# One selection over seven score tiles in place of two interleaved groups, in the odd layer of a hybrid decoder

## The chip, the cores and the metric

The kernel runs on one core of one Trainium2 chip. The metric is the device time of one execution in microseconds; the median of the runs shown is compared. The whole program is one launch.

## The reference, cut to what matters

One inference step of a two-layer trunk: 1024 prompt tokens and 32 sample tokens (8 requests of 4) go through the same weights. The odd layer has an indexer-sparse attention. Each query scores all keys with a small indexer, keeps the 256 best of them (129 of the 516 of a sample query), and attends to these alone:

```python
def _dsa_select(iq, iw, ik, qpos, kpos, ksel):
    r = jax.nn.relu(jnp.einsum('bthd,bsd->bhts', iq, ik))
    score = jnp.einsum('bhts,bth->bts', r, iw)
    score = jnp.where(kpos[None, :] <= qpos[:, None], score, NEG)
    val, idx = lax.top_k(score, ksel)
    return idx, val > 0.5 * NEG
...
        idx, valid = _dsa_select(iqb, iwb, ik, qpos, kpos, ksel)
        g = kv[bidx, idx]
        s = jnp.einsum('bthgd,btshd->bhgts', qb, g[:, :, :, 0]) * SCALE
        p = _masked_softmax(s, valid[:, None, None])
        return jnp.einsum('bhgts,btshd->bthgd', p, g[:, :, :, 1])
```

## The kernel before, in words

`trunk` runs the even layer, then the odd one: `dense` (input projection), `dsa`, `dense` (output projection "oo"), norms and feed-forward. The change lies in `dsa` (L1929), the helper `index_scores` (L2027) and the class `Selection` (L2130).

**The tiles.** The prompt has NT = 8 tiles j of 128 queries; a query of tile j sees (j+1)*128 keys. Tiles 0 and 1 see at most 256 keys and need no selection, so `first` = 2. Tiles 2 to 7 have score tiles of 384, 512, 640, 768, 896 and 1024 columns in `best`; the sample queries have one of 32 rows by 544 columns, `best_s`. These are the seven score tiles.

**The selection.** `Selection` finds each row's threshold by a bitwise search of 31 rounds. `start` counts the scores at or above zero, works out signs and ranks in small operations, and writes sign-flipped copies (`flip`). Each round (`step`) sets one bit of the candidate `cand` (L2202), counts for each tile the copies under it (L2210, a compare with an accumulated sum, on DVE), compares the counts with the limits (`keep`, L2215) and takes over the bit (L2216). `link` makes DVE wait for its own last instruction. For tiles marked `on_act` the count is made on ACT instead (`signs`, L2226, a Sign with accumulator): ACT waits for the candidate (`tried`), DVE's `keep` waits for ACT (`signed`). The last round counts all tiles on DVE. `finish` (L2233 to L2247) breaks ties with a running sum and turns the scores in `best` into a mask of 0 and NEG.

**The order.** `index_scores` goes through units (j, head): PE multiplies into one of two PSUM buffers, ACT takes the relu (L2103), DVE adds the weighted heads (L2120, L2122) and the causal mask (L2127). Every engine does its instructions in program order. The seven tiles are in two groups: group 0 is tiles 2 to 5 (2 and 3 counted on ACT), group 1 is tiles 6, 7 and the sample (7 on ACT); `half` = 6. In `index_scores`, from tile 6 on, DVE does group 0's `start` and one round ahead of each of the 12 units. The rest goes into `attend_prompt` (L778), the attention over all tiles. It goes through units u: tile 0 is one unit, tile 1 two, tiles 2 to 7 four each, 27 in all. PE makes the scores of unit u (L846), then turns (L863) and multiplies with the values (L878) the probabilities of unit u-2, in chunks of two key blocks; DVE adds the mask and takes the maximum (L920), `shift` (L928) releases ACT's exponentials (L999), DVE takes the reciprocal (L937), POOL scales (L978), ACT copies the turned chunks (L989), and DVE copies each tile's result out (L954). Scores of unit u wait for the mask step of two blocks before (two PSUM banks). `beside`, called ahead of `mask(u)` on DVE, and `beside_act` on ACT put the rounds in: beside tiles 0 and 1 the other 19 rounds of group 0 and its `finish`; beside tiles 2 to 5 group 1's `start`, 31 rounds and `finish`. Then SP, which waits for `chosen_sem`, fetches 32 pages of the key/value cache (L670) into the room that the selections used; `attend_samples` (from L1061) reads them behind `attend_prompt`.

Of the kernel before, what the change touches and what calls it, by code (L numbers as in the profile page):

```python
# [20 lines left out]
P = 128  # L21
# [1907 lines left out]
def dsa(nc, k, idx_rows):  # L1929


    with Stage(nc, "dsa") as st:
# [43 lines left out]
        index_scores(nc, k, idx_rows, index, iw, causal, best, best_s, first, at, half, selections[0])  # L1976
        pages = gather.rows
        bits = [chosen.bit for chosen in selections]
        chosen_sem = st.sem("chosen")

        def beside(dve, link, j, n, of):

            if j >= half:
                return
            m, lo, hi = (0, 0, first) if j < first else (1, first, half)
            chosen = selections[m]
            work = lambda x: (x * (x + 1) - lo * (lo + 1)) / (hi * (hi + 1) - lo * (lo + 1))
            before = lambda v: round(bits[m] * (work(j) + (work(j + 1) - work(j)) * v / of))
            if j == lo and n == 0 and m == 1:
                chosen.start(dve, link)  # L1990
            for _ in range(before(n), before(n + 1)):
                chosen.step(dve, link)
            if j == hi - 1 and n == of - 1:
                chosen.finish(dve, link)
                dve.sem_inc(chosen_sem, 1)

        def beside_act(act, j, n, of):

            if j >= half:
                return  # L2000
            m, lo, hi = (0, 0, first) if j < first else (1, first, half)
            chosen = selections[m]
            work = lambda x: (x * (x + 1) - lo * (lo + 1)) / (hi * (hi + 1) - lo * (lo + 1))
            before = lambda v: round(bits[m] * (work(j) + (work(j + 1) - work(j)) * v / of))
            for _ in range(before(n), before(n + 1)):
# [21 lines left out]
def index_scores(nc, k, gather, index, iw, causal, best, best_s, first, at, half, chosen):  # L2027


    with Stage(nc, "idx") as st:  # L2030
# [23 lines left out]
        with nc.Block() as block:  # L2054
# [36 lines left out]
            def _(act):  # L2091
# [7 lines left out]
                for n, (j, hh) in enumerate(units):  # L2099
# [4 lines left out]
                    if j >= half:  # L2104
                        chosen.signs(act)

            @block.vector
            def _(dve):
                link = Chain(dve, chain_sem)
                dve.wait_ge(loaded, 16)  # L2110
                for n, (j, hh) in enumerate(units):
                    r = rows(j)
                    if j == half and hh == 0:
                        chosen.start(dve, link)
                    if j >= half:
                        chosen.step(dve, link)
# [13 lines left out]
class Selection:  # L2130
# [10 lines left out]
    @staticmethod  # L2141
# [5 lines left out]
    def __init__(self, st, name, tiles, want, width, room):  # L2147

        flip, hits, self.cum, self.one = room
        self.lo, n = tiles[0][2], len(tiles)  # L2150
        self.want, self.width = want[:, self.lo:self.lo + n], width[:, self.lo:self.lo + n]
        self.tiles, at = [], 0
# [308 lines left out]
```

## Time and profile before

| | us |
|---|---|
| median of 3 runs (lowest, highest) | 3558.7 (3558.47, 3560.22) |
| profiled execution | 3561.3 |
| its span | 3559.7 |
| index scores and 12 rounds, 2162 to 2242 | 80 |
| attention beside the selections, 2242.5 to 2475 | 232 |
| attention of tiles 6 and 7 alone, 2475 to 2539 | 64 |

Over the span PE is busy 88%, DVE 46%, ACT 22%, POOL 7%; the mean granted clock is 0.908. PEclk is the granted TensorE clock as a share of full speed: 1.00 is 2.4 GHz and 0.50 is 1.2 GHz. The stages around the change are read stage by stage, since the mean shares hide that the engines change places. In a timeline row stand the start, the duration, the engine, the line, the operation and its operands, and in brackets the idle time ahead of it and what ended that. Starts are counted from the start of the span.

### The profile page before, as it was taken

The page shows a single profiled execution, that of the slowest core. Times are in us where ns is not written, and L with a number is a line of the kernel's source. Part 1 is how long each engine was busy: PE and PEld are TensorE (multiplying, and loading weights), DVE is VectorE, ACT ScalarE, POOL GpSimd, SP SyncE. Part 2 cuts the span into 40 slices and gives each one's busy share as a digit, 9 for nine tenths or more (in the row PEclk, how much of TensorE's full clock was granted, in tenths as well). Part 3 has the DMA queues.
Part 4 walks back from the last instruction along what each step waited for, and adds up shares of the span by engine and source line. Part 5 has one row for each costly group of instructions (what it writes and reads, how often), then busy time and mean ns, then how long its engine had stood idle before and what let it go on. Part 6 is the DMA issues. An engine that isn't in the chain of part 4 may idle for free. (4 is left out here: it accounts for less than half of the span.)

```text
span 3559.7 us, 49762 instructions
## 1 busy us (share of the span) xinstructions
PE 3117.9 (88%) x19939; PEld 2790.9 (78%) x19939; DVE 1626.1 (46%) x3131; ACT 797.7 (22%) x1551; POOL 248.1 (7%) x279
## 2 busy tenths in 40 slices
PE   8997799969879999999997968155897999999997
PEld 8997566548859999999986955033495999999995
DVE  2112287656444443344344245988335343344335
ACT  2110276523131000000003113454404000000002
POOL 2001000023000000000002720011100000000000
PEclk9999899977889999999998985567898999999998
DMA  6222310131202011111102330000111111001101
GB/s 232 99 86 102 110 38 1 42 123 31 68 12 83 36 49 36 60 36 36 48 1 75 118 105 0 0 1 15 45 36 36 60 48 60 36 36 48 59 13 49
DMA packets 63277, 193.46 MB, mean 54 GB/s; under 512 B 7812, under 2 KB 32292, under 8 KB 53792
## 3 DMA queue, kind: packets, MB, share of 16 engines
q1 hardware_dynamic: 58176, 172.86, 13.8%
q0 software_dynamic: 3904, 12.46, 1.1%
q10 hardware_dynamic: 1008, 5.41, 0.4%
q8 instruction: 145, 2.38, 0.3%
q14 instruction: 44, 0.36, 0.0%
HBM read 159.68 MB, written 35.36 MB: 55 GB/s over the span
## 5 line engine op out<-in xcount | busy, mean ns | idle before, releaser
L163 PE MATMUL f_up<-f_x_high,f_w_high 128*128 128x352 f32 x2112 | 686.3, 325 | 62.6 <-DVE f_x_low L638 48.5
L165 PE MATMUL f_up<-f_x_high,f_w_low 128*128 128x352 f32 x2112 | 681.5, 323 | 0.0
L164 PE MATMUL f_up<-f_x_low,f_w_high 128*128 128x352 f32 x2112 | 681.4, 323 | 0.0
L163 PEld LDWEIGHTS f_up<-f_x_high,f_w_high 128*128 128x128 f32 x2112 | 399.8, 189 | 65.5 <-issue 65.5
L164 PEld LDWEIGHTS f_up<-f_x_low,f_w_high 128*128 128x128 f32 x2112 | 400.4, 190 | 0.0
L165 PEld LDWEIGHTS f_up<-f_x_high,f_w_low 128*128 128x128 f32 x2112 | 400.0, 189 | 0.0
L163 PE MATMUL f_down<-f_h_high,f_w_high 128*128 128x352 f32 x1056 | 344.9, 327 | 14.0 <-DVE f_w_low L157 8.2
L602 DVE TENSOR_TENSOR f_gated<-f_silu,f_up 128x352 f32<-128x352 f32 x132 | 68.8, 521 | 614.5 <-PE f_up L165 590.7
L616 DVE TENSOR_TENSOR xT_sb<-xT_sb,f_down 128x352 f32<-128x352 f32 x480 | 248.5, 521 | 208.1 <-PE f_down L165 208.1
L164 PE MATMUL f_down<-f_h_low,f_w_high 128*128 128x352 f32 x1056 | 342.0, 324 | 0.0
L165 PE MATMUL f_down<-f_h_high,f_w_low 128*128 128x352 f32 x1056 | 341.5, 323 | 0.0
L579 ACT ACTIVATE f_silu<-f_up 128x352 f32<-128x352 f32 x132 | 61.4, 465 | 825.5 <-PE f_up L165 825.5
L163 PE MATMUL pe_acc<-pe_x_high,pe_w_high 128*128 128x352 f32 x648 | 210.2, 324 | 10.4 <-DVE pe_x_low L320 10.4
L163 PEld LDWEIGHTS f_down<-f_h_high,f_w_high 128*128 128x128 f32 x1056 | 200.1, 190 | 20.4 <-DVE xT_sb L616 10.5
L164 PE MATMUL pe_acc<-pe_x_low,pe_w_high 128*128 128x352 f32 x648 | 208.6, 322 | 0.0
L165 PE MATMUL pe_acc<-pe_x_high,pe_w_low 128*128 128x352 f32 x648 | 208.4, 322 | 0.0
L165 PEld LDWEIGHTS f_down<-f_h_high,f_w_low 128*128 128x128 f32 x1056 | 200.3, 190 | 0.0
L164 PEld LDWEIGHTS f_down<-f_h_low,f_w_high 128*128 128x128 f32 x1056 | 200.2, 190 | 0.0
L583 ACT ACTIVATE f_h_high<-f_gated 128x352 fp32r<-128x352 f32 x132 | 65.7, 498 | 508.5 <-DVE f_gated L602 508.5
L157 DVE TENSOR_TENSOR f_w_low<-f_raw,f_w_high 128x2048 fp32r<-128x2048 f32 x66 | 151.3, 2293 | 2.3
L163 PEld LDWEIGHTS pe_acc<-pe_x_high,pe_w_high 128*128 128x128 f32 x648 | 122.3, 189 | 10.8 <-issue 10.4
L163 PE MATMUL po_acc<-po_x_high,po_w_high 128*128 128x352 f32 x336 | 109.2, 325 | 22.2 <-DVE po_x_low L320 22.2
(429 smaller groups left out, 5034.6 us busy)
## 6 DMA issues: line engine op xcount, KB each, us to landing
f_raw<-w SPq DMA_DIRECT2D x66, 1024.0 KB, 4.8
pe<-pe_y SPq DMA_DIRECT2D x27, 528.0 KB, 2.9
pe_raw<-w_in_e SPq DMA_DIRECT2D x27, 512.0 KB, 3.9
po<-po_y SPq DMA_DIRECT2D x14, 528.0 KB, 2.9
po_raw<-w_in_o SPq DMA_DIRECT2D x14, 512.0 KB, 4.2
xT_sb<-xT ACTq DMA_DIRECT2D x4, 1056.0 KB, 11.3
ro_x<-po SPq DMA_DIRECT2D x8, 528.0 KB, 3.7
y<-xT_sb SPq DMA_DIRECT2D x3, 1408.0 KB, 5.2
```

The source lines that it names most:

```text
L157: dve.tensor_tensor(out=low, in0=src, in1=high.bitcast(F32), op=ALU.subtract).then_inc(split_sem, 1)
L163: pe.matmul(out, wh, xh, start=n == 0, stop=False)
L164: pe.matmul(out, wh, xl, start=False, stop=False)
L165: return pe.matmul(out, wl, xh, start=False, stop=n == depth - 1)
L579: act.activation(S[:, n % 2], up[:, 0, c, 0:CH], ACT.Silu).then_inc(activated, 1)
L583: act.activation(H.high[:, slot, n // NCH, cols(c)], G[:, n % 2], ACT.Copy).then_inc(h_high, 1)
L602: dve.tensor_tensor(out=G[:, n % 2], in0=S[:, n % 2], in1=up[:, 1, c, 0:CH], op=ALU.mult).then_inc(gated, 1)
L616: ins = dve.tensor_tensor(out=x, in0=x, in1=down[:, n % 2, 0:CH], op=ALU.add)
```

## The change

`dsa` builds one `Selection` over all seven tiles instead of two. Its tiles 4, 5 and 6 are counted on ACT; 2, 3, 7 and the sample on DVE. No part of it stands in `index_scores` any more. `start`, all 31 rounds and `finish` are put beside the attention of tiles 0 and 1, whose three units carry `start` and 10 rounds, 11 rounds, and 10 rounds with `finish`. Beside tiles 2 to 7 there is nothing. The fetch of the pages waits for that one selection. The copies for all seven tiles (4768 columns) fill most of the room of the pages, so part of the scratch for hits gets memory of its own.

```diff
@@ dsa, L1945-1955
-        half = first + (NT - first + 1) // 2 + 1
-        on_act_too = lambda j: j in (first, first + 1, NT - 1)
-        tile = lambda j, on_act: (best[:, at[j]:at[j + 1]], P, j - first, on_act)
-        groups = [[tile(j, on_act_too(j)) for j in range(first, half)],
-                  [tile(j, on_act_too(j)) for j in range(half, NT)] + [(best_s[:], NEW, NT - first, False)]]
-        room = Selection.room(st, gather.rows[:].rearrange("p n c -> p (n c)"),
-                              max(sum(tile[0].shape[-1] for tile in tiles) for tiles in groups))
-        selections = [Selection(st, f"g{n}", tiles, want, width, room) for n, tiles in enumerate(groups)]
+        on_act_too = lambda j: j in (first + 2, first + 3, first + 4)
+        tiles = [(best[:, at[j]:at[j + 1]], P, j - first, on_act_too(j)) for j in range(first, NT)] + [(best_s[:], NEW, NT - first, False)]
+        chosen = Selection(st, "sel", tiles, want, width, gather.rows[:].rearrange("p n c -> p (n c)"))
...
@@ dsa, L1976-2009
-        bits = [chosen.bit for chosen in selections]
+        bits = chosen.bit
         chosen_sem = st.sem("chosen")
+        work = lambda j, v, of: round(bits * (j * (j + 1) + 2 * (j + 1) * v / of) / (first * (first + 1)))
         def beside(dve, link, j, n, of):
-            if j >= half:
+            if j >= first:
                 return
...
-            if j == lo and n == 0 and m == 1:
+            if j == 0 and n == 0:
                 chosen.start(dve, link)
-            for _ in range(before(n), before(n + 1)):
+            for _ in range(work(j, n, of), work(j, n + 1, of)):
                 chosen.step(dve, link)
-            if j == hi - 1 and n == of - 1:
+            if j == first - 1 and n == of - 1:
                 chosen.finish(dve, link)
                 dve.sem_inc(chosen_sem, 1)
         def beside_act(act, j, n, of):
...
+            for _ in range(work(j, n, of), work(j, n + 1, of)) if j < first else ():
                 chosen.signs(act)
         def fetch(sp):
-            sp.wait_ge(chosen_sem, len(selections))
+            sp.wait_ge(chosen_sem, 1)
             gather.fetch(sp, k, "cache_dkv")
@@ index_scores, L2103-2116
-                    if j >= half:
-                        chosen.signs(act)
...
-                    if j == half and hh == 0:
-                        chosen.start(dve, link)
-                    if j >= half:
-                        chosen.step(dve, link)
@@ Selection, L2138-2156
-    def room(st, free, width):
...
-        return free[:, 0:width], free[:, width:2 * width], free[:, 2 * width:2 * width + SEQ], st.sb("one", [P, 1])
+        total = sum(tile[0].shape[-1] for tile in tiles)
+        self.cum, rest = free[:, total:total + SEQ], free[:, total + SEQ:]
+        hits = st.sb(f"{name}_hits", [P, total - rest.shape[-1] + SEQ])
+        self.one = st.sb(f"{name}_one", [P, 1])
...
-            self.tiles.append((m, rows, w, score, flip[0:rows, at:at + w], hits[0:rows, at:at + w], on_act))
+            where = 0 if used[0] + w <= rest.shape[-1] else 1
+            spare = (rest, hits)[where][:, used[where]:used[where] + w]
+            used[where] += w
+            self.tiles.append((m, rows, w, score, free[0:rows, at:at + w], spare[0:rows], on_act))
```

## Rows read from the trace of the kernel before

**Rows 1.** windows: busy us (count) of PE, PEld, DVE, ACT, POOL; PEclk; DMA; GB/s
```profile
2162.00:2190.00 28.00, 25.70 (x56) 13.65 (x56) 15.65 (x27) 10.89 (x21) 0.00 (x0) 0.50 0.00 0
2190.00:2242.00 52.00, 26.25 (x45) 9.08 (x44) 49.21 (x125) 25.30 (x60) 0.00 (x0) 0.50 0.00 0
2242.50:2319.50 77.00, 10.52 (x52) 6.92 (x52) 69.29 (x198) 32.24 (x98) 2.84 (x8) 0.50 0.00 0
2319.50:2475.00 155.50, 87.03 (x500) 48.92 (x500) 134.70 (x409) 78.39 (x166) 23.91 (x36) 0.68 0.00 1
2475.00:2539.00 64.00, 60.50 (x504) 36.62 (x504) 26.40 (x92) 40.71 (x75) 20.51 (x20) 0.97 0.23 67
```

**Rows 2.** timeline of DVE (start, us, instruction): one round of group 0
```profile
2244.94 0.17 DVE L2202 TENSOR_SCALAR dsa_g_cand<-dsa_g_thr 128x4 uint32<-128x4 uint32 x1
...
2245.14 0.88 DVE L2210 TENSOR_SCALAR_CACHE_REDUCE dsa_odd_kv<-dsa_odd_kv,dsa_g_cand 128x640 f32<-128x640 f32 x1
...
2245.95 1.01 DVE L2210 TENSOR_SCALAR_CACHE_REDUCE dsa_odd_kv<-dsa_odd_kv,dsa_g_cand 128x768 f32<-128x768 f32 x1
...
2247.40 0.17 DVE L2202 TENSOR_SCALAR dsa_g_cand<-dsa_g_thr 128x4 uint32<-128x4 uint32 x1
```

**Rows 3.** timeline of DVE: counts of other widths, from the last rounds
```profile
2295.55 0.61 DVE L2210 TENSOR_SCALAR_CACHE_REDUCE dsa_odd_kv<-dsa_odd_kv,dsa_g_cand 128x384 f32<-128x384 f32 x1
...
2451.26 1.28 DVE L2210 TENSOR_SCALAR_CACHE_REDUCE dsa_odd_kv<-dsa_odd_kv,dsa_g_cand 128x1024 f32<-128x1024 f32 x1
...
2452.45 0.76 DVE L2210 TENSOR_SCALAR_CACHE_REDUCE dsa_odd_kv<-dsa_odd_kv,dsa_g_cand 32x544 f32<-32x544 f32 x1
```

**Rows 4.** timelines: ACT with accumulator at 640 and 896; DVE's wait for it
```profile
2385.47 0.83 ACT L999 ACTIVATE dsaa_scores<-dsaa_scores,dsaa_shift 128x640 f32<-128x640 f32 x1 [2.87 <-DVE dsaa_shift L928]
...
2481.24 1.03 ACT L999 ACTIVATE dsaa_scores<-dsaa_scores,dsaa_shift 128x896 f32<-128x896 f32 x1
...
2263.83 0.16 DVE L2215 TENSOR_TENSOR dsa_g_keep<-dsa_g_count,dsa_g_limit 128x4 uint32<-128x4 f32 x1 [2.70 <-ACT dsa_odd_kv L2226]
```

**Rows 5.** timelines of PE, ACT, DVE: index scores and their end
```profile
2186.00 4.05 PE L2080 MATMUL idx_acc<-odd_oT 64*128 64x512 f32 x8 [0.20 <-ACT idx_r L2103]
...
2190.36 3.35 PE L2080 MATMUL idx_acc<-odd_oT 64*128 64x512 f32 x4 [0.31 <-ACT idx_r L2103]
...
2189.39 0.92 ACT L2103 ACTIVATE idx_r<-idx_acc 128x896 f32<-128x896 f32 x1 [2.74 <-PE idx_acc L2080]
...
2242.48 0.17 DVE L2202 TENSOR_SCALAR dsa_g_cand<-dsa_g_thr 128x4 uint32<-128x4 uint32 x1 [0.54 <-PEq L2054]
```

**Rows 6.** timeline of DVE: bounds of both finishes and of group 1's start
```profile
2299.00 0.17 DVE L2233 TENSOR_SCALAR dsa_g_ge<-dsa_g_thr 128x4 f32<-128x4 f32 x1
...
2319.60 0.42 DVE L920 CUSTOM_DVE_ANT_0 dsaa_scores<-dsaa_scores_acc,dsa_causal 128x256 f32<-128x256 f32 x1 [0.19 <-DVE dsa_best L2247]
...
2321.53 0.06 DVE L2167 MEMSET dsa_g_count<- 128x3 f32 x1 [0.18 <-DVE dsaa_weight L937]
...
2329.55 0.17 DVE L2202 TENSOR_SCALAR dsa_g_cand<-dsa_g_thr 128x3 uint32<-128x3 uint32 x1
...
2453.65 0.17 DVE L2233 TENSOR_SCALAR dsa_g_ge<-dsa_g_thr 128x3 f32<-128x3 f32 x1
...
2473.97 0.56 DVE L920 CUSTOM_DVE_ANT_0 dsaa_scores<-dsaa_scores_acc,dsa_best 128x384 f32<-128x384 f32 x1 [0.26 <-DVE dsa_best_s L2247]
```

**Rows 7.** timeline of PE: attention's scores after idle, and back to back
```profile
2475.07 3.36 PE L846 MATMUL dsaa_scores_acc<-dsa_rot 64*128 64x512 f32 x8 [23.16 <-DVE dsaa_top L920]
...
2482.40 1.77 PE L846 MATMUL dsaa_scores_acc<-dsa_rot 64*128 64x512 f32 x8
...
2487.63 1.77 PE L846 MATMUL dsaa_scores_acc<-dsa_rot 64*128 64x512 f32 x8
```

**Rows 8.** timelines of DVE and SP: end of attention, fetch of the pages
```profile
2537.91 0.69 DVE L954 COPY odd_oT<-dsaa_o_acc 128x512 f32<-128x512 f32 x1 [9.09 <-PE dsaa_o_acc L878]
...
2476.08 46.19 SPq L670 DMA_DIRECT2D dsa_odd_kv<-cache_dkv  x32
```

More of the change, by code:

```diff
@@ L1975, in dsa @@
                        + [(wT[:, j * P:min((j + 1) * P, T)], iw[0:min(P, T - j * P), j]) for j in range(NT + 1)])
-        index_scores(nc, k, idx_rows, index, iw, causal, best, best_s, first, at, half, selections[0])
+        index_scores(nc, k, idx_rows, index, iw, causal, best, best_s, first, at)
         pages = gather.rows
-        bits = [chosen.bit for chosen in selections]
+        bits = chosen.bit
         chosen_sem = st.sem("chosen")
+        work = lambda j, v, of: round(bits * (j * (j + 1) + 2 * (j + 1) * v / of) / (first * (first + 1)))
         def beside(dve, link, j, n, of):
-            if j >= half:
+            if j >= first:
                 return
[L1985 to L1988, printed above, removed]
-            if j == lo and n == 0 and m == 1:
+            if j == 0 and n == 0:
                 chosen.start(dve, link)
-            for _ in range(before(n), before(n + 1)):
+            for _ in range(work(j, n, of), work(j, n + 1, of)):
                 chosen.step(dve, link)
-            if j == hi - 1 and n == of - 1:
+            if j == first - 1 and n == of - 1:
                 chosen.finish(dve, link)
@@ L1997, in beside_act @@
         def beside_act(act, j, n, of):
-            if j >= half:
[L2000 to L2005, printed above, removed]
+            for _ in range(work(j, n, of), work(j, n + 1, of)) if j < first else ():
                 chosen.signs(act)
         def fetch(sp):
-            sp.wait_ge(chosen_sem, len(selections))
+            sp.wait_ge(chosen_sem, 1)
             gather.fetch(sp, k, "cache_dkv")
@@ L2024, in dsa, with index_scores @@
                 chosen=(rows_of, best_s, lambda pe: pe.wait_ge(loads, 16)))
-def index_scores(nc, k, gather, index, iw, causal, best, best_s, first, at, half, chosen):
+def index_scores(nc, k, gather, index, iw, causal, best, best_s, first, at):
     with Stage(nc, "idx") as st:
@@ L2112, in _ @@
                     r = rows(j)
-                    if j == half and hh == 0:
-                        chosen.start(dve, link)
-                    if j >= half:
-                        chosen.step(dve, link)
                     dve.wait_ge(rectified, n + 1)
@@ L2139, with __init__ @@
     BITS = 31
-    @staticmethod
-    def room(st, free, width):
-        return free[:, 0:width], free[:, width:2 * width], free[:, 2 * width:2 * width + SEQ], st.sb("one", [P, 1])
-    def __init__(self, st, name, tiles, want, width, room):
-        flip, hits, self.cum, self.one = room
+    def __init__(self, st, name, tiles, want, width, free):
         self.lo, n = tiles[0][2], len(tiles)
         self.want, self.width = want[:, self.lo:self.lo + n], width[:, self.lo:self.lo + n]
-        self.tiles, at = [], 0
+        total = sum(tile[0].shape[-1] for tile in tiles)
+        self.cum, rest = free[:, total:total + SEQ], free[:, total + SEQ:]
+        hits = st.sb(f"{name}_hits", [P, total - rest.shape[-1] + SEQ])
+        self.one = st.sb(f"{name}_one", [P, 1])
+        self.tiles, at, used = [], 0, [0, 0]
         for m, (score, rows, _, on_act) in enumerate(tiles):
             w = score.shape[-1]
-            self.tiles.append((m, rows, w, score, flip[0:rows, at:at + w], hits[0:rows, at:at + w], on_act))
+            where = 0 if used[0] + w <= rest.shape[-1] else 1
+            spare = (rest, hits)[where][:, used[where]:used[where] + w]
+            used[where] += w
+            self.tiles.append((m, rows, w, score, free[0:rows, at:at + w], spare[0:rows], on_act))
             at += w
```

## The prediction

> **What bounds the kernel now.** I read first the busy times by stretch [rows 1], because the mean over the span (PE 88%, DVE 46%) tells nothing of the odd layer's attention. There the engines change places. Up to 2190 PE is busy 25.7 of 28 us. From 2190 to 2242, the index scores of tiles 6, 7 and the sample with twelve rounds between them, DVE is busy 49.2 of 52. It stays the bound beside tiles 0 and 1 (69.3 of 77) and beside tiles 2 to 5 (134.7 of 155.5). Behind the last finish PE takes over again: 60.5 of 64 us. So from 2190 to 2475 the time is DVE's queue, and a change is worth what it takes off that queue, less what PE, freed of it, becomes late with. The timelines then give each price: a round [rows 2], the widths it lacks [rows 3], ACT's share [rows 4], and the stretches of start and finish [rows 6].
>
> **Price of a round.** From candidate to candidate a round of group 0 takes 2.46 us [rows 2]. The counts of 640 and 768 columns start 0.81 us apart, and a count holds DVE for its duration less 0.07: 0.81 + 0.94. What is left, 0.71, is fixed: candidate, keep, take-over and the waits between them. Group 1's round (896 and 544 columns) is 2.46 by the same widths. The new round counts 384, 512, 1024 and 544 on DVE: 0.54 + 0.67 + 1.21 + 0.69 [rows 3] (512 lies halfway between 384 and 640), 3.11 with 0.71 fixed: 3.82 us. It replaces one round of each group, 4.92. DVE counts 2464 columns where it counted 2848, and half the fixed part goes.
>
> Does ACT end later? It counts 640, 768 and 896. Nearest rows are exponentials of that width with the same accumulator: 0.83 and 1.03, so 0.93 between them, 2.79 in all [rows 4]. They start 0.20 behind the candidate as DVE's do; with some 0.2 for the last accumulator and the signal they release DVE 3.19 behind it. DVE comes to its keep at 0.20 + 3.11 + 0.11 = 3.42. DVE ends last by 0.2 us; bounds for the round are 3.82 and, were ACT 0.5 us later, 4.1.
>
> **Index scores without rounds.** DVE's queue from 2190 on holds start (some 8 us) and 12 rounds (29.5); both leave. Then PE sets the pace, at two units in 4.36 us for 896 columns [rows 5], and 4.89 for 1024 by the same step per width. The second pair of tile 6 starts at 2190.4, those of tile 7 at 2194.7 and 2199.6. The first relu of a pair comes 3.4 us behind the pair's start [rows 5], for 1024 columns 3.9, and takes 1.0: 2204.5. Behind it DVE has its last two sums of tile 7 (2.6), the mask (1.3) and the sample's four sums and mask (3.7): it ends at 2212.1 instead of 2241.9 [rows 5]. **-29.8 us.**
>
> **Beside tiles 0 and 1.** Before: 2242.5 to 2319.6, 77.1 us: 18 rounds (44.3), a last round (4.6: 0.7 fixed, 2.95 of counts, 1.0 for two sign flips), finish 20.6 [rows 6], and 7.6 for two mask steps and two waits for ACT, which is busy with tile 0's and 1's exponentials when a round begins (2.70 of it in one row [rows 4]). After:
> start: group 1's is 8.0 [rows 6] and group 0's about the same; 2.4 of that (memory sets, rank) is paid once, so 13.8;
> 30 rounds at 3.82: 114.6;
> a last round: 0.7 + 5.9 of counts over all tiles + 2.0 of flips = 8.6;
> finish: 20.6 + 20.3 [rows 6], less 1.2 paid once, 39.7;
> mask steps and waits: 7.6 as before and some 0.2 more for the longer Sign block.
> Sum 184.5, less 77.1: **+107.4 us.** The mask step of tile 1's second unit, at 2319.6 before, comes at 2212.1 + 0.5 + 184.5 = 2397.1.
>
> **Tiles 1 to 7 without rounds.** From that mask step to the last copy it is 218.3 us before (2537.9 - 2319.6) [rows 6, 8], with 107 of selection in DVE's queue. DVE keeps 1.5 to 2.7 us of work per unit, so PE or the chain through the engines sets the unit. PE's price: from the scores of a tile 6 unit to the next is 5.22 us, 1.71 for the scores and 3.51 for the three chunks of a tile 5 unit [rows 7], 1.17 a chunk of two key blocks. Scores scale with the width; an odd last block costs half a chunk and some 0.4 of waiting for its copy. From the scores of one unit to the next: 3.1 for tile 2, 3.25 where tile 3's scores meet tile 2's chunks, 3.55, 3.8, 4.6, 4.8, 5.0 for tile 5. Over the 14 steps from the second unit of tile 2 to the last of tile 5 this makes 3.3 + 3.1 + 3 x 3.25 + 3.55 + 3 x 3.8 + 4.6 + 3 x 4.8 + 5.0 = 55.1. Ahead of it the pipeline fills: mask, reciprocal, POOL (1.9 + 1.8), turns and values of tile 1 at half clock (4.2) and the scores: 9.0. Behind the last pause the scores took 3.36 us at 2475 and 1.77, for wider ones, at 2482, with PE busy between [rows 7], so I take the rest at full. From the mask step of tile 5's last unit (2473.97 before) to the end nothing changes except that PE is not starting cold behind a pause: 63.9 before, 64.6 by the steady step (two steps of 5.2 instead of 3.3 and 6.4). Sum 9.0 + 55.1 + 64.6 = 128.7, **-89.6 us.**
>
> Is the chain shorter than PE's step? Mask to shift to reciprocal 1.5, POOL 1.2, a signal 0.1: 2.8 us for tile 2 against 3.1. It holds, narrowly. If it does not, each of the 16 units of tiles 2 to 5 costs up to 1 us more (+16); if the copy waits are hidden too, it is 3 less.
>
> **Small edits.** The fetch of the pages took 46.2 us on SP's queue [rows 8] and was over at 2522, before the attention's end at 2538; it now starts at about 2395 beside tiles 1 to 5 and ends far ahead of its reader. Nothing else is on SP there. It gains nothing since it was hidden; uncovered it would cost 46. Hits in other memory cost nothing that a row shows. With no rounds beside tiles 2 to 5 nothing waits behind them; with 10 rounds ahead of mask(0), PE's scores and POOL idle longer, but their work is made up while DVE is in its queue.
>
> **Sum.** -29.8 + 107.4 - 89.6 = -12.0 us. DVE's queue loses 37 us (30 rounds x 1.10, and 4 at the starts, finishes and last rounds), and 25 of it turns into DVE idle behind PE. Against the profiled execution's 3561.3 this is 3549.3; the median of the runs shown is 2.6 lower, so I predict 3546.7.
>
> **A rule against a row.** In the index scores PE is busy 25.7 of 28 us and the granted clock stays 0.50 (1.2 GHz) [rows 1]. The Trainium skill, "TensorE: Matmul & The Clock Gate", section "The HAM clock gate", says that the throttled state is the default and that activity releases it; here it did not, so the row decides for me. By the rule the undisturbed matmuls of tiles 6 and 7 would be released.
>
> **Rivals.** (1) *Index scores at full clock.* The pause of PE at 2194 goes. If the clock rises, DVE becomes the bound of tiles 6, 7 and sample with its own 15.1 us from 2189.9: end at 2205, 7 us more gain, 3540. For: the stage becomes denser. Against: it was dense from 2162 to 2190 at 0.50. (2) *The chain sets tiles 2 to 5*, by up to 1 us a unit: 3555 to 3563, no difference. For: POOL's result and ACT's copy are each within 0.5 us of PE's step. Against: tiles 6 and 7 leave PE 60.5 of 64 us. (3) *ACT ends the round*: 0.3 us x 30, 3556. For: a margin of 0.2. (4) *Slower: half clock in tiles 2 to 5.* Behind 150 us of nearly idle PE the clock is 0.50; if it stays there, chunks and scores take 1.8 times as long (3.36 against 1.77) [rows 7], and the 55.1 us become 98: 3590. It decides from about 28% of these steps at 1.2 GHz (12.0 of 43). For: 0.68 in the stretch 2319.5 to 2475, 0.50 in the index scores. Against: 0.97 from 2475 on, when PE was as dense as it will be here. (5) *The edit brings nothing*: if the two groups' rounds were hidden behind PE anyway; 3559. Against: DVE's 134.7 of 155.5.
>
> **How the numbers follow.** A measurement tells 0.2% (7.1 us) from no change; that is 3551.6 to 3565.8. Forecast (3542 to 3551) 0.62; index scores at full clock 0.14; chain late 0.09; ACT last 0.04; nothing 0.02; half clock 0.09. Faster 0.76, same 0.15, slower 0.09. The range 3537 to 3559 takes in the first five.
>
> **What would show it.** L2202 only 31 times, 3.8 us apart; no L2226 row before the attention; index scores ending near 2212; the keep (L2215) waiting for ACT only in two rounds; the mask step of tile 1's second unit near 2397; DVE idle behind PE's scores in tiles 2 to 5, with POOL's wait behind DVE shorter; the last L954 near 2526; PEclk near 1.0 from 2405. Wrong if rounds are over 4 us, if PE waits for POOL's L978 in every unit, or if PEclk is 0.5 there.

## The result, and the profile after

| | before | after |
|---|---|---|
| median of 6 runs each, us | 3564.9 | 3542.6 |
| lowest, highest | 3558.5, 3570.6 | 3535.0, 3547.0 |
| profiled execution, us | 3561.3 | 3547.0 |

The ratio is 0.9936, with a 95% interval of 0.9916 to 0.9955: the change makes the kernel faster. The medians lie 22.3 us apart. The prediction was 3546.7 (12.0 us faster), range 3537 to 3559. Executions of one kernel differ by 10 to 20 us, so the stages are compared in the traces, where most of them repeat within 1 us.

The windows of the kernel after (columns as in [rows 1], which they answer):

```profile
2162.00:2190.00 28.00, 25.90 (x74) 16.88 (x75) 11.93 (x17) 8.88 (x18) 0.00 (x0) 0.50 0.00 0
2190.00:2215.00 25.00, 18.61 (x81) 9.78 (x78) 20.88 (x31) 11.29 (x14) 0.00 (x0) 0.84 0.00 1
2215.00:2405.00 190.00, 12.03 (x56) 7.35 (x56) 174.18 (x478) 97.66 (x221) 6.51 (x16) 0.51 0.01 3
2405.00:2467.00 62.00, 61.58 (x510) 36.80 (x507) 33.97 (x136) 43.53 (x99) 21.69 (x30) 0.99 0.21 61
2467.00:2530.00 63.00, 58.11 (x478) 35.20 (x477) 22.28 (x74) 37.00 (x68) 18.70 (x18) 0.97 0.01 2
```

DVE has one closed block, 174 of 190 us, in which PE does next to nothing. From 2405 on PE is busy 61.6 of 62 us, where before it was 87.0 of 155.5. The granted clock reads 0.84 in the second window: in the index scores it was 0.50 throughout in the kernel before.

DVE's timeline of the kernel after, one round (start, us, instruction), beside [rows 2, 3]:

```profile
2229.08 0.17 DVE L2182 TENSOR_SCALAR dsa_sel_cand<-dsa_sel_thr 128x7 uint32<-128x7 uint32 x1
2229.29 0.61 DVE L2190 TENSOR_SCALAR_CACHE_REDUCE dsa_odd_kv<-dsa_odd_kv,dsa_sel_cand 128x384 f32<-128x384 f32 x1
...
2229.83 0.74 DVE L2190 TENSOR_SCALAR_CACHE_REDUCE dsa_odd_kv<-dsa_odd_kv,dsa_sel_cand 128x512 f32<-128x512 f32 x1
...
2230.49 1.28 DVE L2190 TENSOR_SCALAR_CACHE_REDUCE dsa_sel_hits<-dsa_odd_kv,dsa_sel_cand 128x1024 f32<-128x1024 f32 x1
...
2231.69 0.76 DVE L2190 TENSOR_SCALAR_CACHE_REDUCE dsa_sel_hits<-dsa_odd_kv,dsa_sel_cand 32x544 f32<-32x544 f32 x1
...
2232.50 0.17 DVE L2195 TENSOR_TENSOR dsa_sel_keep<-dsa_sel_count,dsa_sel_limit 128x7 uint32<-128x7 f32 x1
...
2232.90 0.17 DVE L2182 TENSOR_SCALAR dsa_sel_cand<-dsa_sel_thr 128x7 uint32<-128x7 uint32 x1
```

From candidate to candidate it is 3.82 us, the forecast's figure, with the counts 0.54, 0.66, 1.20 and 0.70 apart. ACT's timeline of the same round ends its last count at 2232.15, 0.35 us ahead of `keep`:

```profile
2231.03 1.03 ACT L2206 ACTIVATE dsa_sel_hits<-dsa_odd_kv,dsa_sel_cand 128x896 f32<-128x896 f32 x1
2231.96 0.19 ACT L2206 ACTIVATION_READ_ACCUMULATOR dsa_sel_hits<-dsa_odd_kv,dsa_sel_cand 128x1 f32 x1
```

So ACT doesn't end the round. The waits of DVE over the selection say the same: `keep` (L2195) waited for ACT in two of 30 rounds, 4.1 us in all.

```profile
DVE dsa_sel_keep L2195 <- ACT dsa_sel_hits L2206: 4.1, 2, 2.8
```

DVE's timeline of the kernel after, where it hands over to PE, and the end (beside [rows 6, 8]):

```profile
2396.28 0.42 DVE L920 CUSTOM_DVE_ANT_0 dsaa_scores<-dsaa_scores_acc,dsa_causal 128x256 f32<-128x256 f32 x1 [0.19 <-DVE dsa_best_s L2227]
...
2406.08 0.56 DVE L920 CUSTOM_DVE_ANT_0 dsaa_scores<-dsaa_scores_acc,dsa_best 128x384 f32<-128x384 f32 x1 [3.11 <-PE dsaa_scores_acc L846]
...
2409.55 0.56 DVE L920 CUSTOM_DVE_ANT_0 dsaa_scores<-dsaa_scores_acc,dsa_best 128x384 f32<-128x384 f32 x1 [2.15 <-PE dsaa_scores_acc L846]
...
2458.74 0.56 DVE L920 CUSTOM_DVE_ANT_0 dsaa_scores<-dsaa_scores_acc,dsa_best 128x384 f32<-128x384 f32 x1 [1.34 <-PE dsaa_scores_acc L846]
...
2523.41 0.69 DVE L954 COPY odd_oT<-dsaa_o_acc 128x512 f32<-128x512 f32 x1 [9.07 <-PE dsaa_o_acc L878]
```

2396.28 is the mask step of tile 1's second unit. The idle time of 3.11 us ahead of 2406.08 is the pipeline filling; 2458.74 is the mask of tile 5's last unit, and 2523.41 the last copy.

**Stages.** Four marks cut the stretch: the first sum of the index scores (2164.07 before, 2169.75 after), the end of their last mask, the start of the mask step of tile 1's second unit, the start of the last copy. In us, with a second profile of each kernel (from the experiments):

| stage | before | before, 2nd | after | after, 2nd | forecast |
|---|---|---|---|---|---|
| index scores | 77.9 | 77.9 | 41.3 | 46.2 | -29.8 |
| to tile 1's second unit | 77.7 | 77.7 | 185.3 | 185.3 | +107.4 |
| tiles 1 to 7 | 218.3 | 219.2 | 127.1 | 126.0 | -89.6 |
| sum | 373.8 | 374.7 | 353.7 | 357.5 | -12.0 |

Between the means of the two pairs the sum falls by 18.7 us. The change edits no instruction ahead of the first mark or behind the last copy, yet the kernel's time has both in it. What follows the last copy takes between 1016 and 1028 us in the fourteen profiles of this study, with no order between the kernels. The first mark does show an order: it lies at 2159 to 2165 in the two profiles of before, with group 0 out, in both with `start` in the index scores and without a selection, and at 2166 to 2172 in the eight others, which have all rounds of the selection ahead of tile 2. The difference arises in the first 100 us of the kernel, in the even layer's input projection, where DVE splits the weights for PE. The same instruction, before and after:

```profile
94.14 1.23 DVE L157 TENSOR_TENSOR pe_w_low<-pe_raw,pe_w_high 128x1024 fp32r<-128x1024 f32 x1
```

```profile
101.89 1.23 DVE L157 TENSOR_TENSOR pe_w_low<-pe_raw,pe_w_high 128x1024 fp32r<-128x1024 f32 x1
```

In after DVE had waited 24.2 us for one transfer of weights just ahead of it, and PE was busy 6.7 us of the ten from 75 to 85, all ten in before. Over the eight profiles this instruction comes 2.5 to 7.8 us later than in before; in the others it agrees within 0.5 us. The prediction has no term for it, and no run tells why a transfer that the edit doesn't touch lands later. So the profiled executions differ by less than the stages (spans of 3559.7 and 3555.4 us against 3545.4 and 3547.5, 11.1 us between the means), while the medians differ by more; whether the executions without a profile lose this time too isn't known.

### The profile page after: what moved, and what is told of

Its sections match the earlier page's. It is cut to its first block and busy times, and to the rows that moved or that the text cites. A ratio compares the mean times of both kernels' runs of the same rounds, so it can differ in the third digit from the quotient of the medians.

```text
span 3545.4 us, 49618 instructions
## 1 busy us (share of the span) xinstructions
PE 3081.1 (87%) x19939; PEld 2776.5 (78%) x19939; DVE 1595.6 (45%) x3018; ACT 808.0 (23%) x1551; POOL 244.6 (7%) x279
## 3 DMA queue, kind: packets, MB, share of 16 engines
q1 hardware_dynamic: 58176, 172.86, 13.8%
## 5 line engine op out<-in xcount | busy, mean ns | idle before, releaser
L863 PE MATMUL dsaa_turn<-ident_sb,dsaa_scores 128*128 128x128 f32 x288 | 50.4, 297 | 97.7 <-POOL dsaa_scores L978 97.3
## 6 DMA issues: line engine op xcount, KB each, us to landing
xT_sb<-xT ACTq DMA_DIRECT2D x4, 1056.0 KB, 11.1
```

What stands on the lines that cost most here:

```text
L863: mm = pe.transpose(turn[0:w, c % 2, at:at + P], rows[:, g * ni + i, kt * P:kt * P + w], k.ident[:])
```

## The experiments

### Both kernels once more

No edit; a second profile of the kernel before, and of the kernel after with more runs.

> The kernel before, a second execution profiled. Theory A (the index scores became shorter because the rounds left them: 77.9 us before, 41.3 us after): the index scores last 77 to 79 us again. For the clock in them there are two readings: the first profile of before had its matmul pairs of 896 keys at 4.05 us (half clock) where after had them at 2.47 us, with the same instructions ahead of both. If that difference is an accident of the execution, a second profile may show the pairs at 2.5 us here too, and the last stretch of the index scores is then no shorter, since VectorE ends it; if it is due to the change, they stay at 4.0 us. Ahead of the index scores the time may move by some 6 us either way, as it did between the two profiles (2164.07 and 2169.75 us at the first sum).

> The kernel after, again, for a sharper ratio and a second profile. From the first pair of profiles the four stages of the change give 20.2 us (index scores 36.6 less, beside tiles 0 and 1 107.6 more, tiles 1 to 7 91.2 less), so ratio 0.9943; the first medians gave 22.8 us, ratio 0.9936. Expected 0.992 to 0.996. If the full clock in the index scores was an accident, a profile without it shows them 5 to 7 us longer (the 29.8 us of the prediction instead of 36.6).

Before: 3557.0 us in one run, index scores 77.86 us, pairs of 896 keys at 4.06 us again. After: median 3546.3 of 9 runs against 3565.4 (23 runs of before), 19.1 us apart; ratio 0.9943 (0.9925 to 0.9962), which is 20.3 us of 3565.4. The second profile of after had half clock for longer. Its PE timeline:

```profile
2188.03 4.05 PE L2066 MATMUL idx_acc<-odd_oT 64*128 64x512 f32 x8 [0.20 <-ACT idx_r L2089]
...
2196.75 4.14 PE L2066 MATMUL idx_acc<-odd_oT 64*128 64x512 f32 x8 [0.20 <-ACT idx_r L2089]
2201.60 2.90 PE L2066 MATMUL idx_acc<-odd_oT 64*128 64x512 f32 x8 [0.71 <-ACT idx_r L2089]
```

The clock rose while the pair at 2196.75 ran (1024 keys, 4.14 us) and the next took 2.90. In the first profile of after the pair of 896 keys that answers to 4.05 in [rows 5] took only 2.47:

```profile
2191.68 2.47 PE L2066 MATMUL idx_acc<-odd_oT 64*128 64x512 f32 x8 [0.20 <-ACT idx_r L2089]
...
2197.22 2.79 PE L2066 MATMUL idx_acc<-odd_oT 64*128 64x512 f32 x8 [0.20 <-ACT idx_r L2089]
2200.32 1.12 PE L2066 MATMUL idx_acc<-odd_oT 64*128 64x512 f32 x2 [0.30 <-ACT idx_r L2089]
```

So the index scores of after take 41.3 to 46.2 us, by when the clock rises. Whether the change has to do with that, the next experiments say.

### Group 0 out of the index scores; both groups ahead

The change has three parts that can be done one behind the other: no rounds in the index scores, group 1 moved ahead of tile 2, and one selection instead of two. The first two are built here. ACT's `signs` move along with the rounds.

```diff
@@ index_scores (first kernel)
-                    if j == half and hh == 0:
-                        chosen.start(dve, link)
-                    if j >= half:
-                        chosen.step(dve, link)
@@ beside: group 0 starts beside tile 0
-            if j == lo and n == 0 and m == 1:
+            if j == lo and n == 0:
```

> First of three parts: group 0's start and first 12 rounds leave the index scores and run beside tiles 0 and 1; group 1 stays beside tiles 2 to 5. Theory A (each stage is set by VectorE's queue or, in the index scores, by the pace of the three engines in turn): index scores 30 to 37 us shorter, beside tiles 0 and 1 longer by the start 8.3 and 12 rounds of 2.46 = 29.5, 37.8 us; sum 0 to 8 us slower, ratio 1.000 to 1.002. Rival B (the gain of the whole change comes from taking the rounds out of the index scores): this kernel is 20 us faster, ratio 0.994.

```diff
@@ beside (second kernel, on top of the first; ScalarE's part alike)
+            for at_step in range(work(j, n, of), work(j, n + 1, of)) if j < first else ():
+                chosen = selections[at_step // bits[0]]
+                if at_step % bits[0] == 0:
+                    chosen.start(dve, link)
+                chosen.step(dve, link)
+                if at_step % bits[0] == bits[0] - 1:
+                    chosen.finish(dve, link)
```

> Second part on top: both groups, still two, run one after the other beside tiles 0 and 1, none beside tiles 2 to 5, 62 rounds of 2.46 to 2.48 us. Theory A: beside tiles 0 and 1 some 37 us more than in the kernel after (62 x 2.47 = 153.1 against 31 x 3.82 = 118.4 is 34.7, and a second start's and finish's small instructions 3), so 14 to 22 us slower than before, ratio 1.004 to 1.006; tiles 1 to 7 as in after, 127 us. Rival B (placement alone brings the gain, merging is worth little): as fast as after, ratio 0.994. The kernel after then differs from this one by the merging alone, 37 us by theory A.

| | before | group 0 out | both ahead | after (both profiles) |
|---|---|---|---|---|
| index scores | 77.9 | 42.9 | 46.2 | 41.3, 46.2 |
| to tile 1's second unit | 77.7 | 115.7 | 222.3 | 185.3, 185.3 |
| tiles 1 to 7 | 218.3 | 219.1 | 126.7 | 127.1, 126.0 |
| sum | 373.8 | 377.6 | 395.2 | 353.7, 357.5 |
| ratio to before | | 1.0018 (1.0005, 1.0031) | 1.0054 (1.0038, 1.0069) | 0.9943 (0.9925, 0.9962) |

Theory A held in every column, and both rivals fell. Moving group 0 out of the index scores trades 35.0 us against 38.0: nothing gained. Moving group 1 ahead as well costs 106.6 and gives back 92.4. (3.4 of the 17.6 us by which the sum grows in this second step come from the clock in the index scores, which rose later in this profile.) What makes the change faster is the merging: 222.3 against 185.3 us, 37.0 off DVE's queue at one stroke. Two rounds of the kernel with both groups ahead, DVE's timeline:

```profile
2350.76 0.17 DVE L2187 TENSOR_SCALAR dsa_g_cand<-dsa_g_thr 128x3 uint32<-128x3 uint32 x1
...
2353.24 0.17 DVE L2187 TENSOR_SCALAR dsa_g_cand<-dsa_g_thr 128x3 uint32<-128x3 uint32 x1
```

A round of group 1 is 2.48 us there, of group 0 2.46: 4.94 for the pair against 3.82. Merging here means two things: the fixed part of 0.71 us is paid once and not twice, and ACT counts 384 columns more, DVE 384 fewer (2464 for 2848), which is the other 0.41 of the 1.12. No run takes the two apart.

### The pause in the index scores

The kernel before with group 0's `start` left in the index scores and its first 12 rounds moved beside tiles 0 and 1; two executions profiled.

```diff
@@ index_scores
                     if j == half and hh == 0:
                         chosen.start(dve, link)
-                    if j >= half:
-                        chosen.step(dve, link)
```

> The kernel before with group 0's start left at its place in the index scores (8.3 us of VectorE in one piece, 26 us behind the first sum) and its first 12 rounds moved beside tiles 0 and 1. For the clock in the index scores: in six of seven profiles without start and rounds there the granted clock rose within 21 to 29 us or so of the first sum and the pairs of 1024 keys took 2.6 to 2.9 us; in two later ones only 34 us behind it; in both profiles of before never. Theory C (what keeps the clock down in before is that PE stands still while VectorE is at the start and the rounds): PE pauses some 6 us here, and if it had not risen yet, it stays at half, pairs of 896 and 1024 keys near 4.1 and 4.6 us, index scores some 46.2 + 6 = 52 us. Rival (before's half clock is an accident of two executions): pairs at 2.6 to 2.9 us, index scores 42.9 + 6 = 49 us or less. In time near group0_out's: 3565 to 3575 us.

> The same kernel as start_in_index, a second execution profiled, since the clock's rise differs from one to the next: by theory C both show half clock behind the pause, by its rival at least one shows pairs of 1024 keys at 2.9 us.

3565.1 and 3565.5 us; the index scores took 52.4 us in both. In both, PE's matmuls of 1024 keys stayed at half clock; of the second, PE's timeline:

```profile
2194.47 9.63 PE L2080 MATMUL idx_acc<-odd_oT 64*128 64x512 f32 x16 [4.61 <-ACT idx_r L2103]
2204.25 0.74 PE L2086 MATMUL idx_acc<-ident_sb,idx_kept 128*32 128x128 f32 x5 [0.15 <-ACT idx_r L2103]
```

Sixteen matmuls take 9.63 us, 4.8 a pair, where the pairs of 1024 keys took 2.8 and 2.9 above. Only the transposes behind them run fast (0.74 us for five against 1.2 at half clock).

The granted clock itself says more than the pairs do. In both profiles it rose to 1.00 just as PE came to its pause, and fell back before PE went on: up at 2192.8 and down at 2196.2 in the first (30.0 and 33.4 us behind the first sum), up at 2190.1 and down at 2193.5 in the second (30.7 and 34.1). The windows of the second show it beside PE's busy time (columns as in [rows 1]):

```profile
2186.00:2190.00 4.00, 3.86 (x8) 1.46 (x7) 3.52 (x17) 0.45 (x1) 0.00 (x0) 0.50 0.00 0
2190.00:2194.00 4.00, 0.00 (x0) 0.00 (x0) 3.86 (x10) 0.50 (x1) 0.00 (x0) 0.93 0.00 0
2194.00:2198.00 4.00, 3.53 (x7) 2.16 (x8) 3.90 (x4) 1.33 (x2) 0.00 (x0) 0.50 0.00 0
```

PE idled through the fast stretch and paid half clock behind it. In the ten profiles without `start` and rounds in the index scores the clock rose 21.7 to 35.3 us behind the first sum, held until PE's last matmul of 1024 keys, and the last pair of them took 2.90 us. In the two of before it stayed at 0.50 through the whole stage. So Theory C stands for what comes behind the pause: the pause that `start` puts into PE (here 4.6 and 4.8 us, 6.1 in before) throws the clock back or keeps it down, and the change takes the pause away. It doesn't say why the clock was late in all four. Up to the pause PE has the same work in all fourteen; by 29.7 us behind the first sum, where before's pause begins, the clock had risen in seven of the ten and in none of the four. That may be chance, and no run decides it.

### No selection

The kernel after without `start`, rounds and `finish`: tiles 2 to 7 take the raw index scores as masks.

> The kernel after without its selection: start, rounds and finish are left out, so tiles 2 to 7 take the raw index scores as their masks. Theory A (VectorE's queue sets everything beside tiles 0 and 1, PE everything from tile 1's second unit on): the stretch from the end of the index scores to tile 1's second unit falls from 185.3 us to some 10 us, and tiles 1 to 7 stay near 127 us less the 8 us of refilling, so about 175 to 185 us faster than after, near 3362 us. Rival: part of tiles 2 to 7 is set by VectorE too or by a clock that only rises there; then they differ by more than 10 us.

3364.3 us in one run, 183 less than the profiled run of after (174 of them in the three stages). To tile 1's second unit 8.4 us instead of 185.3, tiles 1 to 7 128.3 against 127.1. The windows of this kernel:

```profile
2207.00:2224.00 17.00, 11.29 (x56) 7.66 (x56) 6.49 (x41) 9.51 (x35) 4.64 (x12) 0.60 0.11 31
2224.00:2308.00 84.00, 83.05 (x697) 49.95 (x696) 44.34 (x173) 60.59 (x132) 31.32 (x42) 1.00 0.16 46
2308.00:2344.00 36.00, 34.39 (x308) 21.43 (x304) 12.62 (x42) 22.53 (x40) 10.89 (x10) 1.00 0.00 1
```

From tile 2 on PE is busy 83.1 of 84 us at clock 1.00: tiles 2 to 7 have no time left in them that a selection takes, and the whole selection, 177 us, stands in front of them uncovered. One part of the expectation failed: the 8 us for refilling the pipeline did not go. From the mask step of tile 1's second unit to that of tile 2's it took 11.2 us here and 9.8 in after.

### Four tiles on ScalarE

```diff
-        on_act_too = lambda j: j in (first + 2, first + 3, first + 4)
+        on_act_too = lambda j: j in (first, first + 2, first + 3, first + 4)
```

> ScalarE counts four tiles (384, 640, 768, 896) instead of three, VectorE three (512, 1024, 544). Theory A (the engine that ends its counts last sets the round; after: VectorE's counts end 3.38 us behind the candidate's start, ScalarE's 3.07): ScalarE then ends at 3.07 + 0.65 = 3.72, and the keep step follows some 0.1 behind, so a round of 4.2 to 4.3 us instead of 3.82, 30 x 0.43 = 13 us slower than after, with every keep step waiting for ScalarE. Rival (VectorE's instruction count sets the round whatever ScalarE does): 3.2 us a round, 18 us faster.

3550.8 us in one run; the stage to tile 1's second unit 197.2 us, 11.9 more than in after, a round 4.18 us. Theory A held, with 0.36 us a round for the expected 0.43. The waits of DVE in this kernel, with `keep` behind ACT in every round:

```profile
DVE dsa_sel_keep L2195 <- ACT dsa_sel_hits L2206: 32.2, 30, 3.9
```

The wait is 0.92 us in an ordinary round: what DVE saves by counting one tile less it stands waiting for ACT.

### The finish split over the attention's tiles

In after, 29.8 us of `finish` (five instructions for each tile from 3 on and the sample) are done before tile 2 needs its own. They are moved between the units of the later tiles, each tile's before its first unit.

```diff
+        late = [(first + t, n) for t, share in enumerate(((2, 1, 1, 1), (1, 1, 1, 2), (1, 2, 2, 2), (2, 2, 2, 3), (2, 2)))
+                for n, x in enumerate(share) for _ in range(x)]
...
             if j >= first:
+                here = [x for x, at_unit in enumerate(late) if at_unit == (j, n)]
+                for x in here:
+                    chosen.write(dve, link, 1 + x // 5, x % 5, x % 5 + 1)
+                if here and here[-1] == len(late) - 1:
+                    dve.sem_inc(chosen_sem, 1)
...
                 chosen.finish(dve, link)
-                dve.sem_inc(chosen_sem, 1)
+                chosen.write(dve, link, 0)
```

> The finish is split: its head and tile 2's five instructions stay at the end of tile 1, the other 30 instructions (29.8 us of VectorE: 3.8, 4.5, 5.2, 5.8, 6.5, 3.9) run between the units of tiles 2 to 6, each tile's own before its first unit; the page fetch starts behind the last. Theory A (VectorE has nothing to spare beside tiles 0 and 1, and has 1.3 us or more in each unit from tile 2 on, where PE sets the pace): 25 to 30 us faster than after, 45 to 52 us faster than before, ratio 0.986 to 0.987. Rival (a unit whose mask is 2 us late stalls PE, since PE is never more than two score blocks ahead): the tiles become longer by 10 to 20 us, and the kernel is only 10 to 20 us faster than after. Second rival: the fetch of 46 us ends behind the last tile and the sample part waits.

The second kernel has also another share: `on_act_too` is `first + 2, first + 3, first + 5`.

> As the split kernel, and ScalarE counts the tiles of 640, 768 and 1024 columns, VectorE 384, 512, 896 and 544. Theory A: VectorE's counts shorten by 0.13 us a round, ScalarE's lengthen by 0.10 (3.17 us behind the candidate, VectorE's 3.25), so the round is 3.69 us and 30 rounds 3.9 us shorter: ratio to the split kernel 0.9989. Rival (ScalarE's end then sets the round): no gain, or 1 to 2 us slower.

Split: 3530.1 us, ratio 0.9920 (0.9901, 0.9939). With the new share: 3521.7, ratio 0.9892 (0.9870, 0.9914). The stage to tile 1's second unit fell by the full 29.8 us (155.5) and by another 3.1 with the new share (152.3; rounds of 3.69 us, as expected; the 8 us between the two medians are more than the stages show, which is about 1: tiles 1 to 7 took 2.0 us more with the new share). But tiles 1 to 7 took 141.1 us in the split kernel instead of 127.1, half of the gain. Tiles 2 to 6, from the first mask of each to that of the next: 15.8, 14.7, 21.7, 25.3, 23.7 us, against 17.2, 12.8, 16.5, 19.2, 23.3 in after. So theory A was wrong in size and the first rival right, though not by the wait it names. The second rival fell: the fetch ended at 2501.5, 6.5 us ahead of the last copy. PE never waited for a mask (L920) from tile 2 on; it waited for POOL's scaling, ten times and 11.0 us behind the one long wait for the selection (none in after). POOL's timeline of the split kernel, one unit of tile 5:

```profile
2432.05 4.84 POOL L978 TENSOR_SCALAR dsaa_scores<-dsaa_scores,dsaa_weight 128x768 f32<-128x768 f32 x2 [3.85 <-DVEq L943]
```

DVE's timeline of the same kernel, at the same moment:

```profile
2432.05 2.29 DVE L2237 TENSOR_TENSOR_SCAN dsa_odd_kv<-dsa_sel_one,dsa_sel_hits 128x1024 f32<-128x1024 f32 x1
2434.37 1.75 DVE L2239 SCALAR_TENSOR_TENSOR dsa_odd_kv<-dsa_odd_kv,dsa_sel_left,dsa_sel_hits 128x1024 f32<-128x1024 f32 x1
```

And PE's, whose idle time ends with POOL's scaling:

```profile
2436.95 0.90 PE L863 MATMUL dsaa_turn<-ident_sb,dsaa_scores 128*128 128x128 f32 x4 [2.64 <-POOL dsaa_scores L978]
```

The two scalings of 768 columns take 4.84 us and end at 2436.89, 0.77 us behind DVE's scan and compare. POOL's timeline of the kernel after has the same two in 1.78:

```profile
2461.51 1.78 POOL L978 TENSOR_SCALAR dsaa_scores<-dsaa_scores,dsaa_weight 128x768 f32<-128x768 f32 x2 [3.01 <-DVEq L943]
```

DVE's compare (L2239) is longer too, 1.75 against 1.28 us at the end of tile 1 in after. The groups of POOL's instructions with their mean durations (ns, the second number behind the bar), in the split kernel:

```profile
L978 POOL TENSOR_SCALAR dsaa_scores<-dsaa_scores,dsaa_weight 128x768 f32<-128x768 f32 x8 | 13.4, 1691 | 12.1 <-DVEq L943 12.1
```

The same group of the kernel after:

```profile
L978 POOL TENSOR_SCALAR dsaa_scores<-dsaa_scores,dsaa_weight 128x768 f32<-128x768 f32 x8 | 7.2, 908 | 12.5 <-DVEq L943 12.5
```

A scaling of 768 columns is 1691 ns in the one, 908 in the other, and 910 in before, where DVE counted rounds beside tile 5. So the counts of the rounds don't disturb POOL, and the instructions of `finish` do. Those with one input are no exception: at 2425.71, beside the last step of one tile and the first of the next (L2244, L2235, both with one input; the second took 1.17 us instead of 0.75), two scalings of 640 columns took 2.49 us, 1.58 in after. The Trainium skill, "SBUF — State Buffer", section "SBUF: two separate sides", says that VectorE and GpSimd share one pair of ports, taken as a whole by a two-input VectorE operation (or one in a two-port mode) or by the GpSimd operation, whichever comes first, with the other blocked until it ends. The rows agree: 4.84 us against 1.78, begun together with the scan and ended only behind the compare. The granted clock has a part in it as well: in the split kernel it fell to 0.50 from 2423.6 to 2427.0 and from 2437.2 to 2440.6, where in after it was 1.00 from 2406.4 to the end of the attention. PE was busy in both stretches, so this is at most 3.4 us of the 14. No run here moved these instructions off POOL's time alone, so how much of the rest is POOL's lengthening and how much the later reciprocal is not separated.

### Paced otherwise, and freed from the fetch

Both have the new share. The first hands out 0, 4, 2, 1 in tile 2, one in each unit of tiles 3 and 4, 1, 1, 1, 2 in tile 5, 4, 4, 2 in tile 6. The second also gives the late instructions scratch that the page fetch doesn't write, starts the fetch at the end of tile 1, and goes on with 1, 1, 1, 2 in each of tiles 6 and 7:

```diff
+        hits, cum, flip = (self.own[0:r, n * SEQ:n * SEQ + w] for n in range(3))
...
                 chosen.write(dve, link, 0)
+                dve.sem_inc(chosen_sem, 1)
```

> The kernel with the split finish and ScalarE's new share, with the 30 late instructions handed out otherwise: 0, 4, 2, 1 in the units of tile 2, one in each unit of tiles 3 and 4, 1, 1, 1, 2 in tile 5, and 4, 4, 2 in tile 6. In the split kernel's profile tiles 4 and 5 took 5.2 and 6.1 us more than in after, tile 3 took 2.0 us more and tile 6 0.4, and PE's score blocks waited for VectorE's masks. Theory A (a unit from tile 4 on has some 1.5 to 2.2 us to spare on VectorE, and what exceeds it stalls PE one for one; tile 6 has more): 5 to 9 us faster than with the first pacing, ratio to before 0.986 to 0.988. Rival (any instruction in front of a mask stalls PE by its own length in tiles 4 and 5, whatever the unit has to spare): tiles 3 to 5 keep 10 us, 3 us gained at most. The page fetch, 46.2 us, starts some 4 us later against the attention's end than in the split kernel, where it ended 6.5 us ahead of the last evacuation.

> The split finish with ScalarE's new share, and the late instructions' three scratch rows in memory that the page fetch doesn't write. The fetch (46.2 us) can so start at the end of tile 1, as in the kernel after, and the 30 late instructions are no longer tied to it: 0, 4, 2, 1 in the units of tile 2, one in each unit of tiles 3 and 4, 1, 1, 1, 2 in each of tiles 5, 6 and 7, each tile's own still before its first unit. Theory A (what an instruction ahead of a mask takes beyond what the unit has to spare stalls PE, and four in one unit of tile 6 were the rest of the loss): tiles 2 to 6 take 95 to 97 us against 101.5 in repaced and 103.2 in split_share, tile 7 its 36.2, so 5 to 8 us faster than both, ratio to before 0.986 to 0.988. Rival (the time went to the fetch or to the clock, not to the place of the instructions): tiles 2 to 6 stay at 101 us.

Repaced: 3529.5 us, ratio 0.9893 (0.9875, 0.9911), the same as before the repacing. Tiles 4, 5 and 6 took 18.3, 25.8 and 25.7 us, against 22.7, 25.3 and 23.6 with the first pacing and the same share. Tile 4 gained 4.3 and tile 3 0.4, but four instructions in one piece (6.7 us) in front of tile 6's first unit lost most of it again; tiles 1 to 7 together took 139.7 us against 143.1. So the gain of 5 to 9 us did not come, and theory A's account of the units did better than its size: tile 4, with an instruction of its own in each unit, is only 1.8 us longer than in after, which speaks against the rival. That PE's score blocks had waited for VectorE's masks, as the expectation says of the split kernel, is wrong by the waits above. DVE's timeline shows the last two of them and the mask they held up:

```profile
2437.98 1.74 DVE L2239 SCALAR_TENSOR_TENSOR dsa_odd_kv<-dsa_odd_kv,dsa_sel_left,dsa_sel_hits 128x1024 f32<-128x1024 f32 x1
2439.76 1.28 DVE L2242 SCALAR_TENSOR_TENSOR dsa_sel_hits<-dsa_best,dsa_sel_cut,dsa_odd_kv 128x1024 f32<-128x1024 f32 x1
2441.08 0.69 DVE L920 CUSTOM_DVE_ANT_0 dsaa_scores<-dsaa_scores_acc,dsa_best 128x512 f32<-128x512 f32 x1
```

Own room: 3522.6 us against 3568.9 for before, ratio 0.9872 (0.9849, 0.9895). Tiles 2 to 6 took 95.5 us, as expected (95 to 97), and tiles 1 to 7 134.1; with 152.5 ahead this is 25 us faster in the stages than after. Tile 5, which had the piece of four behind it, fell from 25.8 to 20.7 us. The rival fell in the main: the fetch now runs beside these tiles and they are shorter. The clock's part can't be more than 2 us, since it was 1.00 throughout here and at 0.50 for 3.4 us in the repaced kernel. The fetch of 46.2 us starts at 2368.86 and is out of the way:

```profile
2368.86 46.22 SPq L670 DMA_DIRECT2D dsa_odd_kv<-cache_dkv  x32
```

This is the fastest kernel of the study, by the point values 0.9872 against 0.9892 for the split with the new share; the two intervals overlap, so that this last step is faster is shown in the stages and not in the time.

## Why the prediction was right, and where it was off

The time (3542.6) lies in the range, 4.1 us under the forecast; the gain was forecast at 12.0 and is about 19 to 23. That the time came out so near is luck in part: the forecast starts from a median of 3558.7 in three runs of before, and six runs have 3564.9. The same 22.3 us from 3558.7 would have been 3536.4, just under the range.

**What bounds the kernel: right.** DVE's queue set 2190 to 2475; without a selection PE needs 128.3 us from tile 1's second unit on, and the rest is the selection's.

**The round: right to the last digit.** 3.82 us, as worked out from the counts and the fixed part. ACT ended ahead of DVE, and the fourth tile on ACT showed where that margin is gone.

**Beside tiles 0 and 1: right.** +107.6 against +107.4. The start took 13.7 us (forecast 13.8) and the waits for ACT 4.1.

**Tiles 1 to 7: right, one term over-sized.** -91.2 against -89.6. The fill took 9.8 us (9.0), the last part 64.7 (64.6), and the 14 steps between 52.7 instead of 55.1: the allowance for waiting on the copies was too much (PE waited for them 1.8 us in all), a miss that the forecast had allowed for ("3 less"). The chain through POOL did not set the units, and the clock was 0.99 from 2405 on, so rivals (2) and (4) fell.

**Index scores: the mis-sized term.** -29.8 forecast, -31.7 and -36.6 measured. The step that failed is that "the row decides for me" against a clock that by the rule "would be released" in the undisturbed matmuls of tiles 6 and 7. The row showed 0.50 in a stretch that ends in a pause which the change removes, and I read it as if it held without the pause. The rule that activity releases the clock (the Trainium skill, "TensorE: Matmul & The Clock Gate", "The HAM clock gate") came true late in the stage, in all ten profiles without the pause; yet PE was busy 25.9 of 28 us at 0.50 first, and 24.0 of 24 in the stretch ahead of that (2142 to 2166), which that rule doesn't lead one to expect. Rival (1) with its 7 us was thus half true: its full size (6.8 more than forecast) in one profile, 1.9 in the other. My forecast left it at 0.14.

**The sum.** -12.0 becomes -18.7 between the stage sums of two profiles each: 4.3 from the index scores, 2.6 from tiles 1 to 7, 0.2 back in the middle. The medians lie 22.3 apart and, with more runs, 19.1; the profiled executions only 11.1, because of the weights that land later in the first 100 us of after. That term stood in no sum of the forecast.

**Which part brings it.** The forecast's account, 37 us off DVE's queue and 25 of it turned into idle, had the first half exactly (37.0, between the kernel with both groups ahead and after). Of the second half 18 us came about.

## What to carry to other kernels

Where an engine's queue is the bound, moving work along it buys nothing: here the two moves alone made the kernel 0.5% slower, and the gain came from doing 31 wide rounds instead of 62 narrow ones, with more of the columns on the second engine. Price a granted clock by what the engine does in the stretch as it will be, without the pauses that the change removes; here a stretch at 0.50 ahead of a pause told nothing of the matmuls behind it once the pause was gone. Work of VectorE put beside the attention was not free here, although VectorE had time to spare: it cost where it came in one piece longer than the unit's slack, and where it ran against GpSimd's operations. And look at the whole execution too: an edit in the odd layer moved a wait in the first 100 us.

## What the runs showed of the hardware that was not expected

The granted clock of TensorE stayed at 0.50 (1.2 GHz) while PE was busy 25.9 of 28 us in the index scores, and rose to 1.00 later in the same stage, at a point that differed by more than 10 us between executions of the same instructions (21.7 and 34.2 us behind the first sum). Where a pause of 4.6 or 4.8 us lay in that stretch, it rose as PE stopped (30.0 and 30.7) and was back at 0.50 before PE went on. What in these matmuls holds it down for so long, no run tells.

GpSimd's scaling of 768 columns took 0.91 us on the mean where VectorE had counts beside it, and 1.69 where it had the instructions of `finish`, and VectorE's compare of 1024 columns with two inputs from SBUF took 1.75 instead of 1.28 us. One-input instructions of VectorE without an accumulated sum lengthened it too (two scalings of 640 columns 2.49 us instead of 1.58).
